# A hybrid decoder layer on one core: half 1's attention projection moved beside the memory attention, with later ticks for the norms

## The chip, the cores and the metric

The kernel runs on one NeuronCore of one Trainium2 chip. TensorE (PE) multiplies matrices, VectorE (DVE), ScalarE (ACT) and GpSimd (POOL) work on tiles, SyncE (SP) issues the weight loads; POOL issues the other transfers. The metric is device time in microseconds (us) of the whole kernel, the median of several runs.

## The reference, cut to what matters

```python
f = swiglu(rms_norm(x, g1), w_gate, w_up, w_down); x = x + 0.5 * rms_norm(f, p1)
h = rms_norm(x, mix_pre_g)
proj = h @ w_in              # columns: gated DeltaNet q,k,v,z,a,b | attention q,k,v
o_a = gdn_mixer(...)         # 4 heads x 128, chunked delta rule
o_b = dilated_mixer(...)     # 8 heads x 64, three (window, dilation) branches
x = x + rms_norm(concat(o_a, o_b) @ w_out, mix_post_g)
x = x + rms_norm(memory_cross_attention(rms_norm(x, mem_pre_g), rms_norm(mem, mem_kv_g)), mem_post_g)
f = swiglu(rms_norm(x, g2), w_gate2, w_up2, w_down2); x = x + 0.5 * rms_norm(f, p2)
```

x is 1024 tokens by 1024 channels in float32; the inner width of the two FFNs is 2816; memory has 256 tokens. All is float32.

## The kernel before

**Granules.** The tokens are worked in two halves of 512 (half 0 and half 1). Every large product is split into *granules*: one 512 KB piece of a weight matrix, loaded by SP into a ring of three, copied by ACT to a rounded part `w_hi` (L1247) and subtracted by DVE to a rest `w_lo` (L1652). PE forms hi·hi + hi·lo + lo·hi, 24 matmuls of 512 columns for a granule, into one of four PSUM banks called `acc` (column granules, `cgran`, L829 to L831; row granules, `rgroup`, L854 to L856). There are 386 granules in one fixed order, the list `STAGES` (L69 to L76): a name such as `up010a` is FFN 0, half 1, chunk 0, part a; `mix1` is all of w_in for half 1 (29 granules), `q0` and `o0` the query and output products of half 0's memory attention, `out1` the product with w_out.

**Ticks.** Everything that is latency-bound is a *job*, a generator that each engine has in its own version: the norms, the mixer (delta rule, then banded attention) and the memory attention. While an engine works through its granules it advances the current job by one `tick` at fixed places: PE two or three times in a granule (`sub`, `KCUT`, `CUTS`), ACT and DVE behind their part of that granule's w_hi and w_lo. `finish()` runs the rest of a job at once, with no granule matmuls between. The job's PE work goes to four other banks, `side`. An engine's instructions run strictly in this order, so a job's matmul that waits stops the granules behind it.

**Norms.** `norm(r, q)` first adds the result r to x and takes the sums (one tick for each of four token tiles, and three more), then in eight ticks transposes (PE L893), scales (ACT L1416) and subtracts (DVE L1820). `ready(q)` waits for its end before the granules that use it.

**Mixer.** `mixer(h)` has 3 ticks `ab`, 20 ticks for each of 4 chunks (k = 0 to 19), then the last gate, loads, 32 attention units, four `pair` transposes and two `conv` ticks: 129 ticks for half 0 and 162 for half 1, where a unit takes two. In a chunk, k = 2 transposes the output of the chunk before: POOL takes a root (L644), DVE multiplies (L1876), PE transposes (L916, `output_tr`, L913), DVE gates (L1880); then k = 3 goes on with L949. `conv` writes the operand of the product with w_out (ACT L1503, L1506, DVE L2022), and PE waits for it with `pe.wait_ge(delta["mix_lo"], ...)` (L1164, L1187).

**Order around half 1's projection.** PE runs `mix1` with the norm in front of it, `q0` with `mixer(1)` at three ticks a granule, then

```python
            for _ in memory(0, A):
                tick()
```

that is 19 ticks of memory attention in the `acc` banks, each with one of the mixer and no granule; `o0` with mixer ticks; 15 ticks of `norm(3, 6)`, again each with one of the mixer and no granule; then FFN 2 of half 0 (`ffn(1, ha, 0, 2, 2, 3)`, two ticks in an up granule and three in a down granule) with the mixer.

Of the kernel before, what the change touches and what calls it, by code (L numbers as in the profile page):

```python
# [18 lines left out]
ALU = mybir.AluOpType  # L19
# [38 lines left out]
MIX_PARTS = [("c", 12, 1, "a"), ("c", 4, 1, "a"), ("c", 1, 1, "a"), ("c", 8, 1, "ad"), ("r", 4, TT, "adad")]  # L58
# [53 lines left out]


# [18 lines left out]
Q0_SUB = 3  # L132
O0_SUB = 3


def mixer_ticks(h):
    t = [("ab", k, 0) for k in range(3)]
# [26 lines left out]
def hybrid_layer(nc, t):  # L164

    ctx = ExitStack()
    with ctx:
# [53 lines left out]
        qm = (at("qm0", [P, KT, TOK], HA), at("qm1", [P, KT, TOK], CZ))  # L221
        kmT = (at("km0", [P, KT, NMEM], HA + 16 * K), at("km1", [P, KT, NMEM], CZ + 16 * K))
        vm = (at("vm0", [P, 2, D], HA + 24 * K), at("vm1", [P, 2, D], CZ + 24 * K))
# [56 lines left out]
        def norm_ticks(r, q):  # L280
            nt = PRE_TILES[q] if q is not None else TT
            return nt + (3 if r is not None and q is not None else 1)
# [37 lines left out]
        mem_kv_in = sem("mem_kv_in")  # L320
        bias_made = sem("bias_made")
# [85 lines left out]

        def staged(eng, h):

            eng.wait_ge(qkv_stored, 16 * TT * (h + 1))  # L410
            for k in range(3):
                eng.wait_ge(slot_stored[k], 16 * (h + 1) * (3, 3, 2)[k])
# [5 lines left out]
        def _(sp):  # L418
# [75 lines left out]
        def _(pool):  # L494
# [115 lines left out]
            def qkv_store(h):  # L610

                i0 = START[f"mix{h}"] + 17
                for j in range(8):
                    na, nd = EVC[BANK[i0 + j]]
                    pool.wait_ge(acc_act, na)
                    pool.wait_ge(acc_dve, nd)
                    dst = q_dram if j < 4 else k_dram
                    pool.dma_start(dst[h][:, j % 4, :], stage_of[h][:, 4 + j % 3, :]).then_inc(slot_stored[j % 3], 16)
                for k in range(TT):
                    na, nd = EVC[TURNS[f"mix{h}"][k]]  # L620
                    pool.wait_ge(acc_act, na)
                    pool.wait_ge(acc_dve, nd)
                    pool.dma_start(v_dram[h][k], stage_of[h][:, k, :]).then_inc(qkv_stored, 16)
# [84 lines left out]

            keep(pool.memset(half_pow[:], -0.5))
# [25 lines left out]
            qkv_store(0)  # L735
# [7 lines left out]
            pool.wait_ge(pe_done, DONE[START["mix1"] - 1])  # L743
            for _ in norm(2, 5):
                pass

            qkv_store(1)
            pool.wait_ge(pe_done, DONE[START["q0"] - 1])
            pool.wait_ge(kv_made, 32)
            pool.dma_start(kmT[0][:], km_dram).then_inc(mem_kv_in, 16)  # L750
            pool.dma_start(vm[0][:], vm_dram).then_inc(mem_kv_in, 16)
            job[0] = mixer(1)
            tick(Q0_SUB * KT)
# [7 lines left out]
            for _ in norm(3, 6):  # L761
                tick()
# [1396 lines left out]
```

## Time and profile before

| | |
|---|---|
| median of three runs | 2729.25 us (2726.69 to 2729.84) |
| time of the profiled execution | 2725.15 us |
| its span, first to last instruction | 2723.4 us |
| PE busy | 2583.1 us, 95% |
| DVE, ACT, POOL busy | 1222.6, 949.7, 392.9 us |
| mean granted TensorE clock | 0.976 |

The page gives busy time by engine; since matmuls are pipelined, a busy PE is not one at its peak. The granted clock is 1.0 at 2.4 GHz and 0.5 at 1.2 GHz, so a mean between tells how much of a stretch ran at the lower level. In the views below a bracket or a column "idle before" gives how long the engine stood before an instruction and which one released it.

### The profile page before, as it was taken

To read this page: it belongs to the slowest core of one execution; us is meant where nothing else is said; L and a number is where in the kernel's file an instruction comes from. 1 tells how busy PE (TensorE), PEld (TensorE's weight loads), DVE (VectorE), ACT (ScalarE), POOL (GpSimd) and SP (SyncE) were. 2 spreads that over 40 slices of the span, in tenths; PEclk is the share of its full clock that TensorE was granted. 3 is DMA by queue.
4 is the path that set the end of the run, shared out by engine and by line. 5 is a ranking of instruction groups with operands and counts; after the bars stand their busy time and mean duration, and the time that the engine had idled before them with its cause. 6 is when DMAs were issued, how large, how long until landed. Compare 5 with 4: busy or idle time off the path is not lost.

```text
span 2723.4 us, 30946 instructions
## 1 busy us (share of the span) xinstructions
PE 2583.1 (95%) x12464; PEld 2113.1 (78%) x12464; DVE 1222.6 (45%) x1913; ACT 949.7 (35%) x1413; POOL 392.9 (14%) x485
## 2 busy tenths in 40 slices
PE   7999998999899999998998978999999999999996
PEld 7788887877778777786777766777787877888885
DVE  5543335634443444467345544333335435533333
ACT  5422224323232244554222223535434424322221
POOL 1460002002211210031022233000002002100001
PEclk9999999999999999999999988999999999999998
DMA  6543334343122233253430114222134234533331
GB/s 201 179 163 100 93 100 139 93 113 97 55 58 68 62 132 101 74 174 86 127 121 24 60 56 142 75 78 85 55 93 150 83 108 147 170 100 94 101 93 62
DMA packets 318846, 280.01 MB, mean 103 GB/s; under 512 B 12272, under 2 KB 266224, under 8 KB 317680
## 3 DMA queue, kind: packets, MB, share of 16 engines
q1 hardware_dynamic: 297856, 204.56, 25.2%
q0 software_dynamic: 19808, 73.46, 7.5%
q8 instruction: 100, 1.64, 0.2%
q14 instruction: 42, 0.34, 0.0%
q10 hardware_dynamic: 1040, 0.00, 0.0%
HBM read 248.63 MB, written 29.36 MB: 102 GB/s over the span
## 4 chain that ended last, share of the span: by engine, by line
PE 87%; DVE 5%; POOL 4%; issue 2%; DMA 1%; ACT 1%; SPq 0%; ACTq 0%; POOLq 0%; DVEq 0%
PE acc L829 15%; PE acc L831 15%; PE acc L830 15%; PE acc L854 9%; PE acc L856 8%; PE acc L855 8%; PE side L1027 3%; PE side L1053 2%; PE side L967 2%; PE side L982 1%; PE side L1042 1%; PE side L893 1%; POOL rs_pre L551 1%; PE side L973 1%; DMA cT<-v_dram 1%
## 5 line engine op out<-in xcount | busy, mean ns | idle before, releaser
L1652 DVE TENSOR_TENSOR w_lo<-w_raw,w_hi 128x1024 fp32r<-128x1024 f32 x384 | 474.0, 1235 | 614.2 <-ACT w_hi L1247 613.7
L1247 ACT ACTIVATE w_hi<-w_raw 128x1024 fp32r<-128x1024 f32 x384 | 405.4, 1056 | 580.4 <-PE acc L856 318.9
L829 PE MATMUL acc<-ha_hi,w_hi 128*128 128x512 f32 (+2 forms) x968 | 392.4, 405 | 1.3 <-DVE ha_lo L1820 1.3
L829 PE MATMUL acc<-hb_hi,w_hi 128*128 128x512 f32 (+1 forms) x968 | 378.3, 391 | 1.2 <-DVE w_lo L1652 1.2
L831 PE MATMUL acc<-hb_hi,w_lo 128*128 128x512 f32 (+1 forms) x968 | 377.4, 390 | 0.0
L830 PE MATMUL acc<-hb_lo,w_hi 128*128 128x512 f32 (+1 forms) x968 | 377.3, 390 | 0.0
L831 PE MATMUL acc<-ha_hi,w_lo 128*128 128x512 f32 (+2 forms) x968 | 376.1, 388 | 0.0
L830 PE MATMUL acc<-ha_lo,w_hi 128*128 128x512 f32 (+2 forms) x968 | 374.7, 387 | 0.0
L854 PE MATMUL acc<-w_hi,act_hi 128*128 128x512 f32 x704 | 286.3, 407 | 0.0
L856 PE MATMUL acc<-w_lo,act_hi 128*128 128x512 f32 x704 | 276.1, 392 | 0.0
L855 PE MATMUL acc<-w_hi,act_lo 128*128 128x512 f32 x704 | 275.4, 391 | 0.0
L829 PEld LDWEIGHTS acc<-ha_hi,w_hi 128*128 128x128 f32 (+1 forms) x968 | 184.6, 191 | 52.5 <-issue 17.6
L831 PEld LDWEIGHTS acc<-ha_hi,w_lo 128*128 128x128 f32 (+1 forms) x968 | 183.7, 190 | 39.1
L829 PEld LDWEIGHTS acc<-hb_hi,w_hi 128*128 128x128 f32 (+1 forms) x968 | 181.5, 187 | 40.0 <-DVE w_lo L1652 1.6
L831 PEld LDWEIGHTS acc<-hb_hi,w_lo 128*128 128x128 f32 (+1 forms) x968 | 181.3, 187 | 39.1
L830 PEld LDWEIGHTS acc<-hb_lo,w_hi 128*128 128x128 f32 (+1 forms) x968 | 181.4, 187 | 38.3
L830 PEld LDWEIGHTS acc<-ha_lo,w_hi 128*128 128x128 f32 (+1 forms) x968 | 184.6, 191 | 33.1 <-issue 0.5
L854 PEld LDWEIGHTS acc<-w_hi,act_hi 128*128 128x128 f32 x704 | 133.0, 189 | 36.9 <-issue 10.9
L856 PEld LDWEIGHTS acc<-w_lo,act_hi 128*128 128x128 f32 x704 | 132.7, 188 | 28.9
L855 PEld LDWEIGHTS acc<-w_hi,act_lo 128*128 128x128 f32 x704 | 133.1, 189 | 26.6 <-issue 1.4
L549 POOL TENSOR_SCALAR rs_post<-ssq_post 128x1 f32<-128x1 f32 x32 | 15.1, 473 | 723.1 <-ACT junk_z L1389 720.3
L1951 DVE CUSTOM_DVE_ANT_0 arena<-side,arena 128x512 f32<-128x512 f32 (+2 forms) x96 | 51.0, 556 | 148.9 <-PE side L1027 145.3
(329 smaller groups left out, 3506.5 us busy)
## 6 DMA issues: line engine op xcount, KB each, us to landing
w_raw<-in_ffn_w_gate SPq DMA_DIRECT2D x88, 512.0 KB, 3.7
w_raw<-in_ffn_w_up SPq DMA_DIRECT2D x88, 512.0 KB, 3.7
w_raw<-in_ffn_w_down SPq DMA_DIRECT2D x88, 512.0 KB, 3.3
w_raw<-in_w_in SPq DMA_DIRECT2D x56, 512.0 KB, 3.8
x_dram<-xbuf POOLq DMA_DIRECT2D x24, 512.0 KB, 3.0
xbuf<-x_dram POOLq DMA_DIRECT2D x24, 512.0 KB, 5.9
arena<-bias_dram POOLq DMA_DIRECT2D x16, 512.0 KB, 3.6
w_raw<-in_w_out SPq DMA_DIRECT2D x16, 512.0 KB, 3.3
```

Of the source, the lines that this page charges most:

```text
L829: pe.matmul(out, hi[:, k, 0:m], xh[:, k, 0:n], start=(k == 0), stop=False)
L830: pe.matmul(out, hi[:, k, 0:m], xl[:, k, 0:n], start=False, stop=False)
L831: done = pe.matmul(out, lo[:, k, 0:m], xh[:, k, 0:n], start=False, stop=(k == KT - 1))
L854: pe.matmul(out, xh[:, kk, ts], hi[:, k, :], start=(kk == 0), stop=False)
L855: pe.matmul(out, xl[:, kk, ts], hi[:, k, :], start=False, stop=False)
L856: done = pe.matmul(out, xh[:, kk, ts], lo[:, k, :], start=False, stop=(kk == 2 * n - 1))
L967: mm = pe.matmul(pairs_of(SB[0][:, hs], s, 1), arena[:, A_S[v % 2], hs], pairs_of(arena[:, U_, hs], s, 1), start=True, stop=True)
L1027: mm = pe.matmul(score_bank(h, n, hh)[:, 0:m], qbT[rows, p, i * P:(i + 1) * P], k_ring(p)[rows, hh, 0:m], start=True, stop=True)
L1053: mm = pe.matmul(SB[3][:, out_cols(n)], pt_of(n)[:, c * P:(c + 1) * P], v_ring(hd // 2)[:, c, (hd % 2) * AD:(hd % 2 + 1) * AD], start=(c = ...
L1247: act.activation(w_hi[:, j % RING, :], w_raw[:, j % RING, :], ACT.Copy).then_inc(w_hi_ok, 1)
L1652: dve.tensor_tensor(w_lo[:, j % RING, :], w_raw[:, j % RING, :], w_hi[:, j % RING, :].bitcast(F32), ALU.subtract).then_inc(w_lo_ok, 1)
L1951: ins = dve.tensor_tensor_reduce(sbuf[:, hh * TOK:hh * TOK + m], score_bank(h, n, hh)[:, 0:m], bias[:, b0 + hh * TOK:b0 + hh * TOK + m], 1 ...
```

## The change

`mix` is cut in three: `gdn_in` (17 granules), `qk_in` (6) and `kv_in` (2 column granules and a group of 4 row granules). For half 0 they still follow one another. For half 1 the order is now gdn_in, q0, qk_in, o0, kv_in. `memory(0)` runs as the job beside qk_in, at three ticks a granule, in the `side` banks and without the mixer; the norm behind it, `norm(3, 6)`, and the mixer advance together (`both`) beside kv_in at two ticks a granule, and `finish()` runs what is left of that norm. FFN 2 of half 0 then has three ticks in an up granule and two in a down granule.

Keys and values of memory come in pieces into a small ring in xbuf's space (`memory_loads` on POOL); q, k and v of half 1 pass through three slots of `arena`, each freed by its store (`slot_free`); queries of half 0's memory attention lie in oT's space.

Four norms get idle ticks between their sums and their transposes (`SLACK`: 6 for q = 2, 5 and 8, 5 for q = 6). The mixer gets one idle tick before its third `ab` tick (so 130 and 163 ticks). In a chunk the output transpose moves from k = 2 to k = 5, DVE's product for it from k = 1 to k = 4 and the gate from k = 2 to k = 6, in another bank. `up010` is cut after 4 blocks of two granules rather than 3, with two ticks a granule in front of the cut. The norm q = 8 is finished behind dn103 rather than in front.

```diff
-STAGES += [("up010a", up_parts(3)), ("mix0", MIX_PARTS), ("up010b", up_parts(3)), ("dn010", dn_parts(0))]
+STAGES += [("up010a", up_parts(4)), ("gdn0", GDN_PARTS), ("qk0", QK_PARTS), ("kv0", KV_PARTS), ("up010b", up_parts(2)), ("dn010", dn_parts(0))]
...
-STAGES += [("out0", ROW_PARTS), ("mix1", MIX_PARTS), ("q0", [("c", KT, 1, "ad")]), ("o0", ROW_PARTS)]
+STAGES += [("out0", ROW_PARTS), ("gdn1", GDN_PARTS), ("q0", [("c", KT, 1, "ad")]), ("qk1", QK_PARTS),
+           ("o0", ROW_PARTS), ("kv1", KV_PARTS)]
...
+SLACK = {2: 6, 5: 6, 6: 5, 8: 6}
...
-    t = [("ab", k, 0) for k in range(3)]
+    t = [("ab", 0, 0), ("ab", 1, 0), ("idle", 0, 0), ("ab", 2, 0)]
...
+            def both(first, second):
+                for _ in first:
+                    next(second, None)
+                    yield
...
@@ PE, chunk(l, k)
                         chan(1, QN)
-                        if l:
-                            output_tr(n - 1, l - 1)
...
                             tr.then_inc(delta["T_psum"], 1)
+                        elif l:
+                            output_tr(n - 1, l - 1)
...
@@ PE, the order of the work
-            up(ha, 3, 3)
+            up(ha, 4, 2)
             finish()
             ready(3)
-            mix(hb, 2)
+            gdn_in(hb, 2)
+            qk_in(hb, 2)
+            kv_in(hb, 2)
             pe.wait_ge(mask_st, N_CONST)
             job[0] = mixer(0)
-            up(ha, 3, 3)
+            up(ha, 2, 3)
...
-            for _ in memory(0, A):
-                tick()
+            job[0] = memory(0)
+            qk_in(ha, 3)
+            finish()
             pe.wait_ge(memo["out_lo"], 8)
+            job[0] = mix_job
             for _ in range(2):
                 rgroup(hc, 4, TT, O0_SUB)
-            for _ in norm(3, 6):
-                tick()
+            job[0] = both(norm(3, 6), mix_job)
+            kv_in(ha, 2)
+            emptied(TURNS["kv1"][-1])
+            finish()
             ready(6)
-            ffn(1, ha, 0, 2, 2, 3)
+            job[0] = mix_job
+            ffn(1, ha, 0, 2, 3, 2)
             finish()
             pe.wait_ge(delta["mix_lo"], 4)
```

In the excerpts below a row is the line, the operation, what it writes and reads, and its shape; line numbers are each version's own (before: L829 to L831 and L854 to L856 are granules; after: L907 to L909 and L932 to L934).

The first place is PE in chunk 3 of half 1. Before, the transpose of the last chunk's output (L916) stands right behind the transposes of keys and queries (L910).

```order
L855 MATMUL acc<-w_hi,hc_lo 128x512
L856 MATMUL acc<-w_lo,hc_hi 128x512
L910 MATMUL side<-ident,arena 128x128 x8
L916 MATMUL side<-ident,cT 128x128 x4
L854 MATMUL acc<-w_hi,hc_hi 128x512
```

After, it is L1002 and stands behind the first product of the chunk's inversion (L1049), three ticks later.

```order
L908 MATMUL acc<-ha_lo,w_hi 128x512
L909 MATMUL acc<-ha_hi,w_lo 128x512
L1049 MATMUL side<-arena 128x32x2 x4
L1002 MATMUL side<-ident,cT 128x128 x4
L907 MATMUL acc<-ha_hi,w_hi 128x512
```

The second place is PE at the end of half 0's mixer. Before, the last transposes (L1089) have granules of the down product (act_hi) on both sides, 156 more granule matmuls up to the next transposes of a norm, of which the first 60 are still of this down product.

```order
L855 MATMUL acc<-w_hi,act_lo 128x512
L856 MATMUL acc<-w_lo,act_hi 128x512
L1089 MATMUL side<-ident,arena 128x128 x4
L854 MATMUL acc<-w_hi,act_hi 128x512
L855 MATMUL acc<-w_hi,act_lo 128x512
```

After, the last of the down product stands in front of the end of the attention (L1128, L1139) and of these transposes (L1175), and the next row is the product with w_out, whose operand (hb) `conv` writes.

```order
L933 MATMUL acc<-w_hi,act_lo 128x512
L934 MATMUL acc<-w_lo,act_hi 128x512
L1128 MATMUL side<-ident,arena 128x128 x4
L1139 MATMUL side<-cT,arena 128x64 x7
L1175 MATMUL side<-ident,arena 128x128 x4
L932 MATMUL acc<-w_hi,hb_hi 128x512
L933 MATMUL acc<-w_hi,hb_lo 128x512
```

The third place is PE at norm(3, 6). Before, mixer ticks of chunk 3 follow each other without a granule from k = 3 (L949, L950) on, and behind seven of them the norm's transposes (L893) come between.

```order
L950 MATMUL side<-cT 128x128
L956 MATMUL side<-ident,arena 128x128 x4
L967 MATMUL side<-arena 128x32x2 x4
L982 MATMUL side<-arena 128x32x2 x4
L967 MATMUL side<-arena 128x16x4 x4
L973 MATMUL side<-ident,arena 128x128 x4
L982 MATMUL side<-arena 128x16x4 x4
L967 MATMUL side<-arena 128x8x8 x4
L973 MATMUL side<-ident,arena 128x128 x4
L982 MATMUL side<-arena 128x8x8 x4
L893 MATMUL acc<-ident,oT 128x128 x4
```

After, granules of kv_in stand in front of the norm's first transpose (L979), and only its eight ticks are without a granule; the mixer is then at the end of chunk 2 (L1066 at k = 16, L1078 at k = 17) and goes on to k = 3 of chunk 3.

```order
L933 MATMUL acc<-w_hi,ha_lo 128x512
L934 MATMUL acc<-w_lo,ha_hi 128x512
L1049 MATMUL side<-arena 128x64 x4
L1055 MATMUL side<-ident,arena 128x128 x4
L979 MATMUL acc<-ident,oT 128x128 x4
L1066 MATMUL side<-arena 128x64 x4
L979 MATMUL acc<-ident,oT 128x128 x4
L1078 MATMUL side<-state,cT 128x128
```

## Rows read from the trace of the kernel before

**Rows 1.** The page, parts 1, 4 and 5: busy time, chain by engine, one group.

```profile
PE 2583.1 (95%) x12464; PEld 2113.1 (78%) x12464; DVE 1222.6 (45%) x1913; ACT 949.7 (35%) x1413; POOL 392.9 (14%) x485
...
PE 87%; DVE 5%; POOL 4%; issue 2%; DMA 1%; ACT 1%; SPq 0%; ACTq 0%; POOLq 0%; DVEq 0%
...
L1247 ACT ACTIVATE w_hi<-w_raw 128x1024 fp32r<-128x1024 f32 x384 | 405.4, 1056 | 580.4 <-PE acc L856 318.9
```

**Rows 2.** Windows (length; busy PE, PEld, DVE, ACT, POOL; clock): mix0; half 1's attention.

```profile
487.00:644.00 157.00, 157.00 (x694) 127.63 (x693) 76.53 (x112) 47.81 (x65) 5.42 (x10) 1.00 0.39 109
...
1665.00:2001.00 336.00, 331.90 (x1653) 255.41 (x1653) 128.19 (x335) 152.68 (x222) 17.53 (x30) 0.99 0.28 90
```

**Rows 3.** Waits of PE, whole span: us in total, times, longest.

```profile
PE side L916 <- DVE cT L1876: 22.0, 6, 5.1
PE side L893 <- DVE oT L1813: 20.1, 3, 10.4
...
PE side L956 <- DVE arena L1913: 10.7, 8, 3.2
...
PE side L1027 <- DMA cT<-v_dram: 5.6, 2, 3.9
PE side L893 <- DVE xbuf L1813: 5.5, 2, 4.6
PE side L893 <- DVE res_cz L1813: 5.2, 2, 2.6
PE side L1067 <- DVE sm L1992: 4.4, 2, 2.2
```

**Rows 4.** Timeline of chunk 2 of half 0: start, us, engine, line.

```profile
809.30 1.01 POOL L644 TENSOR_TENSOR sm<-sm,half_pow 128x4 f32<-128x4 f32 x1
...
810.34 1.52 DVE L1876 TENSOR_TENSOR cT<-cT,sm 128x512 f32<-128x512 f32 x1 [4.65 <-POOL sm L644]
...
811.92 0.69 PE L916 MATMUL side<-ident,cT 128*128 128x128 f32 x2 [5.07 <-DVE cT L1876]
```

**Rows 5.** Windows around three waits.

```profile
439.00:487.00 48.00, 39.60 (x182) 32.49 (x181) 29.11 (x32) 24.52 (x37) 19.30 (x24) 0.89 0.47 152
...
808.00:816.00 8.00, 4.08 (x13) 3.41 (x14) 3.35 (x3) 2.37 (x3) 3.15 (x4) 0.57 0.00 0
1208.00:1246.00 38.00, 27.56 (x114) 22.49 (x113) 29.79 (x41) 19.41 (x30) 14.01 (x21) 0.87 0.43 130
```

**Rows 6.** Timeline of DVE in the norm q = 3, which starts at 439.

```profile
450.53 1.28 DVE L1802 SCALAR_TENSOR_TENSOR oT<-oT,rs_post,grow_z 128x1024 f32<-128x1024 f32 x1
...
462.06 0.74 DVE L1813 TENSOR_SCALAR oT<-xbuf,rs_pre 128x1024 f32<-128x1024 f32 x1
```

**Rows 7.** Windows: memory attention of half 0; norm(3, 6).

```profile
1457.00:1527.00 70.00, 60.00 (x335) 46.95 (x335) 40.98 (x103) 25.55 (x71) 17.89 (x16) 0.93 0.00 1
...
1613.00:1665.00 52.00, 33.22 (x194) 29.77 (x193) 31.05 (x39) 16.21 (x29) 25.31 (x31) 0.69 0.14 52
1621.00:1652.00 31.00, 18.39 (x85) 16.90 (x84) 18.66 (x21) 10.07 (x20) 18.52 (x23) 0.50 0.22 86
```

**Rows 8.** Timeline at the end of half 0's mixer.

```profile
1144.97 0.27 PE L1089 MATMUL side<-ident,arena 128*128 128x128 f32 x1
...
1145.61 0.60 ACT L1498 ACTIVATE cT<-side 128x512 f32<-128x512 f32 x1 [2.98 <-PE side L1089]
...
1149.39 1.90 ACT L1506 ACTIVATE hb_hi<-cT 128x2048 fp32r<-128x2048 f32 x1
...
1152.58 2.29 DVE L2022 TENSOR_TENSOR hb_lo<-cT,hb_hi 128x2048 fp32r<-128x2048 f32 x1
```

**Rows 9.** ACT at 1671; groups of ACT, 1665 to 1838.

```profile
1672.25 1.28 ACT L1317 ACT_TABLE_LOAD   x1
1673.55 0.60 ACT L1317 ACTIVATE sg<-acc 128x512 f32<-128x512 f32 x1
...
L1459 ACT ACTIVATE arena<-arena,sm 128x640 f32<-128x640 f32 (+3 forms) x17 | 16.7, 982 | 41.2 <-DVE sm L1959 41.2
```

More of the change, by code:

```diff
@@ L281, in norm_ticks @@
             nt = PRE_TILES[q] if q is not None else TT
-            return nt + (3 if r is not None and q is not None else 1)
+            return nt + (3 if r is not None and q is not None else 1) + SLACK.get(q, 0)
         gain_in = [sem("gain_in_mem"), sem("gain_in_ffn1")]
@@ L734, in _ @@
             x_next(t["x"][0], 1, 0, 3)
-            qkv_store(0)
+            for n in range(12):
+                qkv_store(0, n)
             for _ in mixer(0):
@@ L808, in chain, with both @@
                     yield from j
+            def both(first, second):
+                for _ in first:
+                    next(second, None)
+                    yield
             def bank_free(n):
@@ L871, in dn, with gdn_in, qk_in, kv_in @@
                     rgroup((act_hi, act_lo), CH[c] // 2, TT, sub, blk[0] - CH[c])
-            def mix(op, sub):
-                for j in range(25):
+            def gdn_in(op, sub):
+                for j in range(17):
                     cgran(op, sub, TOK, 8 if j == 16 else P)
+            def qk_in(op, sub):
+                for _ in range(6):
+                    cgran(op, sub)
+            def kv_in(op, sub):
+                for _ in range(2):
+                    cgran(op, sub)
                 rgroup(op, 4, TT, sub)
@@ L1236, in chain, with both @@
                     yield from j
+            def both(first, second):
+                for _ in first:
+                    next(second, None)
+                    yield
             def split(j):
@@ L1287, in cplain, with rgroup @@
                     pend[0] = out
-            def rgroup(n, tiles, sub, dst_of):
+            def rgroup(n, tiles, sub, dst_of, before=None):
                 for j in range(n):
@@ L1574, in _ @@
             flush()
-            mix(1, 2)
+            gdn_in(1, 2)
             finish()
             flush()
-            job[0] = mixer(1)
+            mix_job = mixer(1)
+            job[0] = mix_job
             cplain(KT, Q0_SUB, lambda j: qm[0][:, j, :])
             flush()
-            for _ in memory(0, A):
-                tick()
+            job[0] = memory(0)
+            qk_in(1, 3)
+            finish()
+            job[0] = mix_job
             rows_to(oT, 4, O0_SUB)
             flush()
-            for _ in norm(3, 6):
-                tick()
-            ffn(0, 2, 2, oT, 3)
+            job[0] = both(norm(3, 6), mix_job)
+            kv_in(1, 2)
+            flush()
+            finish()
+            job[0] = mix_job
+            ffn(0, 2, 3, oT, 2)
             finish()
@@ L1642, in chain, with both @@
                     yield from j
+            def both(first, second):
+                for _ in first:
+                    next(second, None)
+                    yield
             def split(j):
@@ L1805, in norm @@
                                                  op0=ALU.mult, op1=ALU.add).then_inc(post_x, 1)
-                    if q is not None and s > off:
+                    if q is not None and off < s <= nt + off:
                         k = s - off - 1
@@ L2094, in _ @@
             flush()
-            mix(1, 2)
+            gdn_in(1, 2)
             finish()
             flush()
-            job[0] = mixer(1)
+            mix_job = mixer(1)
+            job[0] = mix_job
             cplain(KT, Q0_SUB, lambda j: qm[0][:, j, :])
             flush()
-            for _ in memory(0, A):
-                tick()
+            job[0] = memory(0)
+            qk_in(1, 3)
+            finish()
+            job[0] = mix_job
             rows_to(oT, 4, O0_SUB)
             flush()
-            for _ in norm(3, 6):
-                tick()
-            ffn(0, 2, 2, oT, 3)
+            job[0] = both(norm(3, 6), mix_job)
+            kv_in(1, 2)
+            flush()
+            finish()
+            job[0] = mix_job
+            ffn(0, 2, 3, oT, 2)
             finish()
```

243 lines of the change are left out of this document (155 added, 88 removed).

## The prediction

> **What bounds the kernel now.** I read the page first: PE is busy 95% of the span and makes 87% of the chain that ended last [rows 1]. Busy is not yet full speed, so I then looked for a stretch that shows what dense work costs: in mix0, 694 matmuls fill 157.00 us at granted clock 1.00 [rows 2], 0.226 us each, and 5.43 us for a granule of 24. The change adds no granule. So its worth lies in what PE loses beside that work, and that has two parts. The first is waits: the waits of PE name them with their releasers [rows 3]. The second comes with them: behind a wait of some 4 us the windows show a stretch at half clock. Around the longest wait for an output transpose it is 0.57 over 8 us, that is 2 x 0.43 x 8 = 6.9 us at 1.2 GHz, of which the wait itself covers about half; the other 3.6 us are work done at half speed, 1.8 us lost [rows 5]. I price each wait so: its length, and half of what PE works in the low stretch.
>
> **The change, gains first.**
>
> (a) *Output transposes.* PE waits for them 22.0 us in 6 waits [rows 3]. The reason is seen in the timeline: POOL's root stands behind three large products, DVE's product (1.52 us) waits for it 4.65 us, and PE 5.07 us for that [rows 4]. Three ticks later the same chain, which overran by 5.1 us at most, has 5.4 to 8.2 us of granules more in front of it, so the wait goes. Five of the waits drew a low stretch at 1.8 us: 22 + 9 = 31. The next step of the chunk still waits for DVE (L956, 10.7 us in 8, [rows 3]) and starts earlier now; I take 2 us back. Gain 29, bounds 12 (half of each wait turns up at L956, and its clock) and 31.
>
> (b) *Norm q = 5.* The longest wait is 10.4 us, 38.0 minus 27.6 in its window, where clock 0.87 means 9.9 us at half speed, about half of it work: 2.5 lost [rows 3, 5]. Six idle ticks at two a granule are 16.3 us, more than the wait. Gain 13.
>
> (c) *Norms q = 2 and q = 8.* 4.6 us and 2.6 us of waits [rows 3], the same cure; with their low stretches 7 and 4. Gain 11.
>
> (d) *Norm q = 3.* It has no slack, but its ticks come two a granule. Before, PE idled 8.4 us here (48.0 minus 39.6, [rows 5]); DVE's last product ended at 462.8 [rows 6], 23.5 us behind the norm's start. PE will now ask for it at the eighth tick, four granules or 21.7 us on: 1.7 us of wait if the chain keeps its pace. It may not: a tile takes 2.5 us of DVE in two products like the one shown, and the last product now stands in the fourth granule's first tick, behind that granule's w_lo. The wait lies between 1.7 and 7.1 (one granule later). I take 5. Gain 3, bounds 1 and 9.
>
> (e) *The idle tick in ab.* 4.4 us in 2 waits (L1067, [rows 3]); a further tick is 1.4 to 2.7 us. With clock, gain 6.
>
> (f) *Memory attention.* Its window of 70 us has 10.0 us of idle PE, and clock 0.93 (9.8 us at half speed, of which I count 7 as work): 13.5 lost, 1.2 of it an output transpose that (a) has [rows 7]. Beside granules 18 of 19 ticks are covered. Left are the last tick and the wait behind it: each an ACT copy like the 0.60 us one [rows 8], a DVE subtraction of 0.7, and hand-overs, 1.9 us, so 4; a low stretch 2; the start (queries just copied, keys just loaded) 1. Gain 5, bounds 0 and 11.
>
> (g) *norm(3, 6).* Of 52 us PE idles 18.8, and from 1621 to 1652 all of its 18.4 us of work ran at 0.50, 9.2 lost: 28 [rows 7]. After, four tiles at 2.5 us on DVE delay mixer ticks beside kv_in: 2. The last v tile waits for a slot's store, and PE for its copy: 2. Then eight ticks stand bare. The fifteen bare ticks of before idled 18.8, or 1.25 each, so 10; since k = 17 to 19 and 0 to 3, each waiting for the one before, are among them, I take 12, and 5 for the clock. Together 21. Gain 7, bounds -5 and 20.
>
> Gains: 29 + 13 + 11 + 3 + 6 + 5 + 7 = 74.
>
> **Then what it costs.**
>
> (h) *End of half 0's mixer.* Before, 6 granules of three ticks in each of up010b and dn010 and 48 of two are 132 ticks for 129. Now up010b has 4: 12 + 18 + 96 = 126 for 130. Four ticks are bare: the last unit, pair, both conv; and the row behind them is the product that waits for conv. This cover is what hid it: before, the chain from the pair transposes (1144.97) to the last subtraction (1152.58 + 2.29) took 9.9 us with a w_hi copy and a w_lo in it [rows 8] and 60 matmuls of the down product (13.6 us) ran meanwhile. Bare it is 0.45 + 0.3 + 0.60 + 2 x 1.90 + 0.2 + 2.29 = 7.6, with the last unit 2.5 ahead and 1.3 of PE's own work off: 8.8, and 2.4 for the clock as in (b). Cost 11, bounds 5 and 14. Queued behind it are all granules of out0.
>
> (i) *End of half 1's mixer.* 24 + 24 + 12 + 8 + 48 x 2 = 164 ticks for 163 (before 166 for 162). The pair transposes stand three ticks, 8.2 us, ahead of out1; the same chain with its w_hi and w_lo takes 9 to 10. Cost 1.
>
> (k) *Loads of the attention.* PE waited 3.9 us for them [rows 3]; three ticks of cover shrink from 8.2 to 5.4 us. Cost 3.
>
> (l) *Attention at three ticks beside up granules.* Before, this stretch lost 4.1 us in 336 [rows 2]. In an up granule with the gate ACT has, ahead of the copy that PE's second tick wants: table load 1.28, silu 0.60 [rows 9], w_hi 1.06 [rows 1], table load 1.28, exp 0.98 [rows 9], the copy 0.60 [rows 8], and 0.3 of hand-over: 6.1 us. PE comes there after 18 matmuls (4.1) and a tick of about 2: 6.1. That is level, in 12 granules, with 0 to 1.5 us of wait each. Cost 4, bounds 0 and 18.
>
> The Trainium skill, ScalarE: Activation LUTs, section What ACT_TABLE_LOAD costs, speaks against this step: it gives 1.28 us for the load and some 1.4 us more for a drain at each switch of set. The trace has the 1.28 us, but the silu starts at 1673.55, 0.02 us behind the load [rows 9], so no drain is paid here. By the page, (l) would be an estimated 33 us (12 x 2.8) and the sum 26.
>
> Costs: 11 + 1 + 3 + 4 = 19. Net 74 - 19 = 55. The profiled execution took 2725.15 us around a span of 2723.4; the sum makes 2670 and 2668 of these. It is 4.1 us under the median of the three runs; from that, 2729.25 - 55 = **2674 us**.
>
> **Rivals.**
>
> *The waits come back one step on.* (a) is worth 12: L956 and the A-block products of POOL wait for the same engines. For it: POOL still takes the root ahead of them. Against it: POOL is done with the root at 810.3, 1.6 us before PE even began that transpose [rows 4], and the product is now wanted three ticks later. Time 2674 + 17 = 2691.
>
> *Better cover than I give.* (h) 5, (l) 0, (d) 9, (f) 9: 6 + 4 + 6 + 4 = 20 us less, 2654.
>
> *Slower: the attention at three ticks.* If the second tick's wait in (l) falls into all 24 up granules, it costs 24 times its length against 59 us of everything else; it is no change at 2.5 us a granule and slower by over 0.2% from (59 + 5.5) / 24 = 2.7. At 3.0, both table loads and a bit on the path, the time is 2729 - 59 + 72 = 2742. For it: ACT's path is as long as PE's. Against it: gate granules are every second one, and dn100 had three ticks in the same stretch with clock 0.99 [rows 2].
>
> *A drain behind table loads,* as a mechanism of ACT in (l): 1.4 us more at each of two loads in 12 granules, 12 x 2.8 = 33 for 4, so 2703; the gap of 0.02 us speaks against it [rows 9]. It is the page's rule, weighed in (l).
>
> *The change does not bring what it names:* bare ticks in (g) as dear as before, and all small returns at their bound, 2715 to 2728. For it: from k = 0 to k = 2 the work goes from PE to ACT, DVE, POOL and DVE before PE has it again, and that stands bare.
>
> **How the numbers follow.** Forecast (2660 to 2688) 0.55; waits come back 0.21; better cover 0.12; little left 0.06; slower 0.04; drain 0.02. The range leaves out the slow rival, the end of little left, and the far ends of the two on either side: 2652 to 2706. A change under 0.2% (5.5 us) is about what a measurement of this kernel can't tell from none. Faster by more 0.93, within 0.03, slower 0.04.
>
> **What the profile after should show.** In the waits of PE the row for the output transposes near zero, and L956 not over 13 us in all; no wait at the norm's transposes of q = 2, 5 and 8, and one of 2 to 7 us at q = 3. Right ahead of out0, a wait of 8 to 9 us for DVE's hb_lo, which did not exist. In the bare ticks behind kv_in 8 to 14 us of waits, the largest for the normed queries at k = 2, and a granted clock under 0.8. The memory attention beside granules at clock near 1.0 but for its end. Most likely to make me wrong: waits at the transposed probabilities all through up100 and up101, or a low clock in the half of the mixer where I expect none.

## The result, and the profile after

The changed kernel takes 2646.80 us (median of 4 runs, 2645.15 to 2647.55) against 2727.97 us (4 runs, 2724.16 to 2729.84): ratio 0.9706, 95% interval 0.9694 to 0.9718, 81 us less. The forecast was 2674, range 2652 to 2706. The direction and most terms hold; the gain is 27 us larger than forecast.

The page of the changed kernel, the rows that answer to [rows 1]:

```profile
PE 2554.3 (97%) x12464; PEld 2090.3 (79%) x12464; DVE 1231.1 (47%) x1913; ACT 936.5 (35%) x1405; POOL 402.9 (15%) x491
...
PE 89%; DVE 5%; POOL 2%; issue 1%; DMA 1%; ACT 1%; SPq 0%; ACTq 0%; DVEq 0%; POOLq 0%
```

PE executes the same 12464 matmuls and is busy 28.8 us less: that is the time saved by matmuls that no longer run at half clock. The span of the profiled executions fell by 77.8 (2723.4 to 2645.6), so the other 49 us are waits.

The waits of PE in the changed kernel, whole span (us in total, times, longest), for [rows 3]:

```profile
PE side L979 <- DVE memx L1941: 11.3, 1, 11.3
PE side L1113 <- DMA cT<-v_dram: 8.3, 2, 7.4
PE side L996 <- DVE arena L2030: 7.2, 6, 3.7
PE side L1038 <- DVE arena L2039: 7.0, 8, 1.8
PE acc L932 <- DVE hb_lo L2148: 7.0, 1, 7.0
PE side L1049 <- DVE arena L2051: 5.1, 2, 2.7
PE side L979 <- DVE oT L1941: 4.4, 2, 2.6
PE side L979 <- DVE res_cz L1941: 2.6, 1, 2.6
```

L979, L1038, L1113 and L1002 are L893, L956, L1027 and L916 of before. The output transposes (22.0 us in 6) have no row any more. Their neighbour L956 (k = 4), which I expected to take some of it over, fell from 10.7 to 7.0. The norms' row for oT fell from 20.1 to 4.4 and the one for res_cz from 5.2 to 2.6. Those for xbuf (5.5 to 0.9) and for ab (4.4 to 0.3) stand further down now. New is hb_lo, 7.0 us in one wait ahead of out0. The loads of the attention grew from 5.6 to 8.3.

Windows of the changed kernel (length; busy PE, PEld, DVE, ACT, POOL; clock; DMA): the norm q = 3; the end of half 0's mixer; the norm q = 5; the memory attention beside granules; the eight bare ticks; the attention's loads; the up granules of chunk 1 of FFN 2 with the attention at three ticks.

```profile
433.00:485.00 52.00, 49.44 (x227) 40.43 (x226) 32.52 (x35) 27.32 (x40) 17.03 (x24) 0.97 0.50 160
1117.00:1131.00 14.00, 6.09 (x30) 4.89 (x29) 7.46 (x8) 7.92 (x9) 2.78 (x5) 0.76 0.12 35
1179.00:1207.00 28.00, 27.04 (x120) 22.06 (x118) 23.27 (x29) 17.41 (x28) 13.52 (x21) 1.00 0.48 151
1347.00:1415.00 68.00, 65.47 (x279) 48.27 (x277) 31.89 (x83) 25.67 (x66) 6.07 (x10) 1.00 0.27 86
1543.00:1569.00 26.00, 18.02 (x136) 16.31 (x136) 15.53 (x24) 11.24 (x18) 10.39 (x12) 0.93 0.10 38
1630.00:1645.00 15.00, 7.64 (x22) 4.84 (x20) 2.45 (x7) 2.21 (x4) 4.00 (x7) 0.66 0.84 302
1746.00:1881.00 135.00, 135.00 (x702) 102.30 (x701) 51.23 (x159) 68.67 (x106) 4.18 (x7) 1.00 0.22 67
```

Read against [rows 5] and [rows 7]: in the memory attention clock 0.93 became 1.00; in the stretch behind o0, 0.69 became 0.93. Only two windows are still low, the end of half 0's mixer and the attention's loads. The last row is dense throughout.

**Where the 78 us came from.** I gave each matmul of both traces the median interval to its successor for matmuls of its kind; what a stretch takes beyond the sum is its loss. (The figures hold to about 1 us, since they depend a little on what counts as one kind; the gains hold better.) The losses of the whole program are 164.6 us before and 86.4 after. By stretch, beside the forecast's terms sorted into the same stretches:

| Stretch | lost before | after | gain | forecast |
|---|---|---|---|---|
| norm q = 2 | 8.9 | 2.0 | 6.9 | 7 |
| norm q = 3 | 10.7 | 4.3 | 6.4 | 3 |
| half 0's mixer to up013 | 41.5 | 13.5 | 28.0 | 20 |
| dn013 and out0 | 2.4 | 13.6 | -11.2 | -11 |
| norm q = 5 | 11.8 | 0.7 | 11.1 | 13 |
| q0 and memory attention | 22.6 | 7.2 | 15.4 | 9 |
| o0, norm(3, 6), bare ticks | 46.1 | 22.2 | 23.9 | 18 |
| chunks 0 and 1 of FFN 2, half 0 | 9.3 | 15.3 | -6.0 | -8 |
| norm q = 8 | 4.2 | -0.5 | 4.7 | 4 |

For the third row the forecast has three output transposes with their clock (12.9 + 5.4), half of (e), and 1 taken back. The surplus sits where the mixer runs beside granules: 8 us in half 0 and 12 in the two stretches of half 1.

### The profile page after: what moved, and what is told of

Read it like the earlier page. It is cut to its first block, busy times and chain, and to the rows that moved or that the text cites. A ratio compares the mean times of both kernels' runs of the same rounds, so it can differ in the third digit from the quotient of the medians.

```text
span 2645.6 us, 30948 instructions
## 1 busy us (share of the span) xinstructions
PE 2554.3 (97%) x12464; PEld 2090.3 (79%) x12464; DVE 1231.1 (47%) x1913; ACT 936.5 (35%) x1405; POOL 402.9 (15%) x491
## 4 chain that ended last, share of the span: by engine, by line
PE 89%; DVE 5%; POOL 2%; issue 1%; DMA 1%; ACT 1%; SPq 0%; ACTq 0%; DVEq 0%; POOLq 0%
PE acc L907 16%; PE acc L909 15%; PE acc L908 15%; PE acc L932 9%; PE acc L934 9%; PE acc L933 9%; PE side L1113 3%; PE side L1139 2%; PE side L1049 1%; PE side L1066 1%; PE side L1128 1%; PE side L1191 1%; PE side L1223 1%; PE side L979 1%; POOL rs_pre L590 1%
## 5 line engine op out<-in xcount | busy, mean ns | idle before, releaser
L1775 DVE TENSOR_TENSOR w_lo<-w_raw,w_hi 128x1024 fp32r<-128x1024 f32 x384 | 488.2, 1272 | 542.5 <-ACT w_hi L1355 542.1
L907 PE MATMUL acc<-ha_hi,w_hi 128*128 128x512 f32 (+2 forms) x968 | 396.0, 409 | 2.8 <-DVE ha_lo L1948 1.1
L907 PE MATMUL acc<-hb_hi,w_hi 128*128 128x512 f32 (+1 forms) x968 | 377.6, 390 | 1.2 <-DVE w_lo L1775 1.2
L909 PE MATMUL acc<-hb_hi,w_lo 128*128 128x512 f32 (+1 forms) x968 | 376.7, 389 | 0.0
L909 PE MATMUL acc<-ha_hi,w_lo 128*128 128x512 f32 (+2 forms) x968 | 374.2, 387 | 0.0
L932 PE MATMUL acc<-w_hi,act_hi 128*128 128x512 f32 x704 | 285.4, 405 | 0.0
L934 PE MATMUL acc<-w_lo,act_hi 128*128 128x512 f32 x704 | 275.1, 391 | 0.0
L907 PEld LDWEIGHTS acc<-ha_hi,w_hi 128*128 128x128 f32 (+1 forms) x968 | 183.3, 189 | 53.1 <-issue 18.6
L909 PEld LDWEIGHTS acc<-ha_hi,w_lo 128*128 128x128 f32 (+1 forms) x968 | 182.6, 189 | 38.9
L907 PEld LDWEIGHTS acc<-hb_hi,w_hi 128*128 128x128 f32 (+1 forms) x968 | 180.9, 187 | 40.1 <-DVE w_lo L1775 1.9
L909 PEld LDWEIGHTS acc<-hb_hi,w_lo 128*128 128x128 f32 (+1 forms) x968 | 180.9, 187 | 38.6
L932 PEld LDWEIGHTS acc<-w_hi,act_hi 128*128 128x128 f32 x704 | 132.3, 188 | 37.7 <-issue 12.2
L934 PEld LDWEIGHTS acc<-w_lo,act_hi 128*128 128x128 f32 x704 | 132.1, 188 | 28.7
```

The costliest lines, as they stand in the source:

```text
L907: pe.matmul(out, hi[:, k, 0:m], xh[:, k, 0:n], start=(k == 0), stop=False)
L909: done = pe.matmul(out, lo[:, k, 0:m], xh[:, k, 0:n], start=False, stop=(k == KT - 1))
L932: pe.matmul(out, xh[:, kk, ts], hi[:, k, :], start=(kk == 0), stop=False)
L934: done = pe.matmul(out, xh[:, kk, ts], lo[:, k, :], start=False, stop=(kk == 2 * n - 1))
L1775: dve.tensor_tensor(w_lo[:, j % RING, :], w_raw[:, j % RING, :], w_hi[:, j % RING, :].bitcast(F32), ALU.subtract).then_inc(w_lo_ok, 1)
```

## The experiments

"Before" is 2726.6 to 2728.4 us in all groups of runs; each ratio is to the runs of before on the same chip, with its 95% interval.

**1. Output transposes alone**, on the kernel before (the edit in short; the transposes also go to another bank).

```diff
# PE, chunk step k
-  k == 2: output_tr(n - 1, l - 1)      k == 3: wait gated
+  k == 5: output_tr(n - 1, l - 1)      k == 17: wait gated
# DVE
-  k == 1: out_norm(n - 1, l - 1)       k == 2: out_gate(n - 1, l - 1)
+  k == 4: out_norm(n - 1, l - 1)       k == 6: out_gate(n - 1, l - 1)
```

> The kernel before, with the output transposes alone moved three steps later in the chunk (their norm and their gate with them). The priced theory (each wait costs its length and half of the work in the half-clock stretch behind it) gives 29 to 33 us less than before: 22.0 of waits, 9 of clock, and nothing or 2 us lost at the step that waits for the normed queries. If the miss of 27 us in the forecast sits in this term (the transposes held back more than their own waits), it gains 45 us or more. If the waits come back one step on, 12 to 17.

Measured 2694.80, ratio 0.9879 (0.9865 to 0.9894), 34 us less. Its profiled span is 28.4 shorter than before's, and by stretch the loss falls 41.5 to 23.8 in half 0's mixer and 46.1 to 33.6 behind the memory attention. Two of its waits of PE:

```profile
PE side L952 <- DVE arena L1911: 11.7, 8, 3.2
PE side L963 <- DVE arena L1923: 11.6, 4, 7.2
```

These two lines are L956 and L967 of before. The first, the next step, grew by 1.0 and the second by 1.2 (from 10.4 in 4). Term (a), 29, holds.

**2. No idle ticks for the norms**, on the changed kernel.

```diff
-SLACK = {2: 6, 5: 6, 6: 5, 8: 6}
+SLACK = {6: 5}
```

> The changed kernel without the idle ticks of the norms q = 2, 5 and 8 (those of q = 6, which pace the merged stretch, stay). The forecast's terms (b) and (c) give 24 us more than the changed kernel, about 2671, with waits at the norm transposes of about 10, 5 and 3 us back. If a wait costs its length alone and the clock is no part of it, 18 us. If the miss sits here, 35 or more.

Measured 2669.91, ratio 0.9791 (0.9775 to 0.9808): 23 us slower than the changed kernel. Its row for the norms reads

```profile
PE side L979 <- DVE oT L1941: 14.7, 3, 10.3
```

The 10.3 us wait is back in full. Terms (b) and (c), 24 together, hold with length plus clock; length alone (18) does not.

**3. The regrouping alone:** the changed kernel with transposes as before, SLACK as in 2, and

```diff
-    t = [("ab", 0, 0), ("ab", 1, 0), ("idle", 0, 0), ("ab", 2, 0)]
+    t = [("idle", 0, 0), ("ab", 0, 0), ("ab", 1, 0), ("ab", 2, 0)]
```

> The changed kernel with everything but the regrouping undone: output transposes back at their old step, no idle ticks for q = 2, 5 and 8, the idle tick of ab put ahead of ab where it parts nothing. What is left is the move of the query, key and value projections of half 1 and the ticks that follow from it. The forecast's terms for it (5 + 7 gained, 19 lost) make it 7 us slower than the kernel before. From the trace of the changed kernel I now expect it 6 to 12 us faster: the memory attention keeps 4 us of waits at full clock, the bare ticks 8 us, and the attention at three ticks costs nothing. If the surplus sits in the other parts, it is within 3 us of the 7 slower.

Measured 2706.19, ratio 0.9919 (0.9904 to 0.9933): 22 us faster than before. Both numbers that I had given, 7 slower and 6 to 12 faster, were wrong. By stretch, 14 us of gain stand in half 0's mixer (41.5 to 27.7), where nothing of the order changes but the place of one block of two granules, and where the output transposes still wait.

**4. The end of half 0's mixer covered**, on the changed kernel, in all three engines.

```diff
-            ffn(0, ha, 1, 4, 2)
+            ffn(0, ha, 1, 2, 2)
+            ffn(0, ha, 2, 3, 2, 3)
+            ffn(0, ha, 3, 4, 2)
```

> The changed kernel with three ticks a granule instead of two in the six down granules of chunk 2 in half 0: 132 ticks for the 130 that the mixer wants, so that none stands bare ahead of out0. If term (h) is right (a bare chain of 7 to 9 us and its clock), the 7.0 us wait for hb_lo goes and the time falls by 8 to 11 us, to about 2637. Rival: three ticks a granule in the attention are dearer in waits than in a down granule of half 1 (0.7 us), and it gains under 4.

Measured 2638.58, ratio 0.9672 (0.9657 to 0.9686): 8 us less than the changed kernel. The row for hb_lo is gone, the loss of dn013 and out0 falls from 13.6 to 2.8, and that of dn012 grows from 2.2 to 3.3. Term (h), 11, holds: 10.8 in the trace. The rest of the way to 8 is given back elsewhere: up100 loses some 2 us more than in the changed kernel and up102a, with the norm q = 7, 1.6.

**5. The split of chunk 0 alone**, on the kernel before (the order in short).

```diff
-up010a 3 blocks at 3 ticks, mix0, up010b 3 blocks at 3 ticks
+up010a 4 blocks at 2 ticks, mix0, up010b 2 blocks at 3 ticks
```

> The kernel before with one thing of the change: chunk 0 of half 0 is split 4 and 2 blocks around the mixer projection instead of 3 and 3, the four blocks at two ticks a granule. Nothing of half 1 moves, no idle tick, transposes at their old step. The forecast's terms (d) 3 gained and (h) 11 lost give 8 us slower than before. My theory now is that the shift of two ticks against the granules takes waits and low clock out of the delta chunks of half 0, 14 us that no term of the forecast held, beside 6.5 gained at the norm q = 3 and 12 lost ahead of out0: 8 us faster than before. If the gain seen in the regrouping alone comes from half 1 only, this one is 5 or more slower.

Measured 2726.35, ratio 0.9995 (0.9986 to 1.0005): no difference. By stretch: q = 3 gains 6.4 (the forecast's 3), dn013 and out0 lose 11.3 (11), and the delta chunks of half 0 gain 2 only. My theory that the shift by two ticks explains experiment 3 fell. Experiment 3 differs from this one in half 0 by one thing, the idle tick ahead of ab.

**6. Four more bare ticks**, on the changed kernel.

```diff
-SLACK = {2: 6, 5: 6, 6: 5, 8: 6}
+SLACK = {2: 6, 5: 6, 6: 9, 8: 6}
```

> The changed kernel with four more idle ticks in the norm q = 6, so that twelve ticks of the mixer stand bare behind the value projection instead of eight. By the forecast's price (1.5 us of wait and 0.6 of clock for a bare tick) 8 us slower than the changed kernel; by what the trace after shows (0.96 us each, hardly any clock) 4 us; less still by 1 to 3 where the later ticks beside FFN 2 are relieved, as the mixer is four ticks further on. If bare ticks draw the clock down once they are many, as in the kernel before (fifteen of them with all work of 30 us at 0.50), 12 us or more, with a granted clock near 0.5 in the stretch.

Measured 2657.04, ratio 0.9739 (0.9725 to 0.9754): 10 us slower than the changed kernel. The window of its bare ticks:

```profile
1543.00:1583.00 40.00, 28.07 (x168) 25.75 (x167) 20.65 (x31) 11.39 (x20) 15.28 (x16) 0.79 0.04 15
```

Before the four ticks, 26 us held 8.0 of idle PE at clock 0.93; now 40 us hold 11.9 at 0.79. A further bare tick costs 1.0 us of wait, but the granted clock is lower, and the loss of the stretch grows by 10.6 from 19.5. So the price of a bare tick is not constant. That their number sets it is argued and not shown, since other steps of the mixer stand bare too (k = 4 to 7 are added).

**7. One idle tick for q = 3, 4 and 7**, on experiment 4.

```diff
-SLACK = {2: 6, 5: 6, 6: 5, 8: 6}
+SLACK = {2: 6, 3: 1, 4: 1, 5: 6, 6: 5, 7: 1, 8: 6}
```

> The kernel with the covered end (three ticks in the down granules of chunk 2, half 0) and one idle tick each for the norms q = 3, 4 and 7, whose transposes still wait 2.6, 1.8 and 2.6 us. Sixteen ticks for sixteen. If the waits and their clock go, 9 us less than with the covered end alone, about 2630. Rival: the last transpose now stands in the last tick, and the copy and the subtraction behind it (0.6 + 0.7 us and hand-overs) stand bare ahead of the next granule, which gives 1.5 to 2 us back at each of three: 4 us or less gained.

Measured 2633.97, ratio 0.9656 (0.9640 to 0.9672): 4.6 us less than experiment 4. The rival is right, as two rows of its waits show:

```profile
PE acc L907 <- DVE hb_lo L1952: 3.1, 2, 1.6
PE acc L907 <- DVE ha_lo L1952: 2.6, 2, 1.6
```

Three waits of 1.56 us stand now where the last transpose's copy and subtraction are bare, in place of 2.6, 1.8 and 2.6. By stretch, against experiment 4, q = 3 and q = 7 gain 2.5 each, while out0, with the norm q = 4, loses 1 us more: that one is not worth its tick.

**8. Cover for the attention's loads**, on experiment 4.

```diff
-    t += [("load", k, 0) for k in range(2)]
+    t += [("load", k, 0) for k in range(2)] + [("idle", 0, 0)] * (3 * h)
-            ffn(1, ha, 0, 2, 3, 2)
+            ffn(1, ha, 0, 1, 3, 2)
+            ffn(1, ha, 1, 2, 3, 3)
```

> The kernel with the covered end and, in half 1, three idle ticks between the loads of the attention and its first scores, paid with three ticks in the six down granules of chunk 1 of FFN 2. If term (k) is the wait of 7.4 us for the keys and values and some 4 us of clock behind it, both go, and it takes 10 to 11 us less than the covered end alone, about 2628. Rival: the down granules at three ticks cost 3 or more, or the loads are slow because they wait for their turn in the queue, not for their length, and a wait stays.

Measured 2632.69, ratio 0.9651 (0.9636 to 0.9665): 5.9 us less than experiment 4, half of what I expected.

```profile
PE side L1113 <- DMA cT<-v_dram: 3.3, 2, 2.6
```

The wait fell from 7.8 to 2.6, not to nothing; the loss of up100 fell from 14.0 to 6.4, and up101 lost 1.0 more. The loads themselves did not change much: the last transfer waited for takes 8.5 us from its issue in the kernel before, 8.1 in the changed one and 8.8 here. It is the cover that differs.

**9 and 10. One idle tick in the kernel before**, ahead of ab, and between its ticks.

```diff
-    t = [("ab", k, 0) for k in range(3)]
+ 9: t = [("idle", 0, 0), ("ab", 0, 0), ("ab", 1, 0), ("ab", 2, 0)]
+10: t = [("ab", 0, 0), ("ab", 1, 0), ("idle", 0, 0), ("ab", 2, 0)]
```

> The kernel before with one idle tick put ahead of the first tick of ab, in both halves; it parts nothing, it only shifts every later tick of the mixer by one against the granules (133 minus 3 is 130 ticks for 132 in half 0, 163 for 166 in half 1). My theory now: this shift alone, not the parting of the ab ticks, takes waits and low clock out of the delta chunks, since at two ticks a granule the odd one falls elsewhere: 12 us less in the chunks of half 0, 3 to 10 in half 1, together 15 to 22 less than before. By the forecast's term (e), which counted only the two ab waits, this kernel is worth nothing, 0 to 2.

> The kernel before with the idle tick where the change has it, between the second and the third tick of ab. The forecast's term (e) says 6 us less than before (4.4 of ab waits and clock). My theory now says this comes on top of the shift: 4 to 6 less than the kernel with the idle tick ahead, 20 to 27 less than before.

Measured 2715.13, ratio 0.9951 (0.9935 to 0.9968), and 2708.93, ratio 0.9933 (0.9918 to 0.9948): 13 and 19 us less than before, each a little short of what my theory gave (15 to 22, and 20 to 27). The parting is worth about 6, as term (e) said. The mere shift by one tick is worth 13 by the medians and 8.2 by the profiled spans, and no term had it. Waits of PE from up010b to up012 in the kernel before:

```profile
PE side L916 <- DVE cT L1876: 12.9, 3, 5.1
PE side L910 <- DVE arena L1902: 4.6, 3, 2.8
PE side L956 <- DVE arena L1913: 3.8, 4, 1.8
```

and in experiment 9:

```profile
PE side L916 <- DVE cT L1876: 9.3, 3, 4.0
PE side L956 <- DVE arena L1913: 3.2, 4, 1.8
...
PE side L910 <- DVE arena L1902: 1.3, 2, 1.0
```

Same work, same steps, 7.5 us less in these rows (a new wait of 0.7 aside): only the place of each step in its granule differs.

**11. No idle tick in half 0**, on the changed kernel.

```diff
-    t = [("ab", 0, 0), ("ab", 1, 0), ("idle", 0, 0), ("ab", 2, 0)]
+    t = [("ab", 0, 0), ("ab", 1, 0)] + [("idle", 0, 0)] * h + [("ab", 2, 0)]
```

> The changed kernel without the idle tick in half 0 only. By term (e) the one ab wait of 2.2 us and its clock come back (3 us) and one bare tick fewer ahead of out0 gives 2 back: 1 us slower. By the shift theory the chunk waits of half 0 come back too, smaller than in the kernel before since the output transposes are out of the way: in all 6 to 10 us slower, about 2654.

Measured 2653.69, ratio 0.9733 (0.9719 to 0.9748): 7 us slower than the changed kernel, where term (e) gives 1. The loss of half 0's mixer is 19.3 instead of 13.5. dn013 and out0 lose the same 13.6: one bare tick fewer there gives nothing back. Of what the mixer loses, some 3.4 stand in up010b, where the ab ticks are, 2.5 in dn010, and nothing in the granules with two ticks. So part of the 7 is the parting, and with the output transposes out of the way the shift is worth less than in the kernel before.

**12. Combined:** the edits of experiments 4, 7 and 8.

> The covered end, the idle ticks for the norms q = 3, 4 and 7, and the cover for the attention's loads, together on the changed kernel. Each alone on the covered end gave 4.6 and 5.9 us; they lie in different stretches, so 10 us less than the covered end alone and 18 to 19 less than the changed kernel, 2627 to 2629. If the shift of two times one tick in half 1 (more idle ticks) costs elsewhere, 2632.

Measured 2627.64, ratio 0.9635 (0.9621 to 0.9650): 19 us less than the changed kernel, as expected. It is the fastest of all, at clock 0.995.

**13 and 14. Two and three idle ticks ahead of ab**, on the kernel before.

```diff
-    t = [("ab", k, 0) for k in range(3)]
+    t = [("idle", 0, 0)] * 2 + [("ab", k, 0) for k in range(3)]      # 14: * 3
```

> The kernel before with two idle ticks ahead of ab in both halves (131 ticks for 132 in half 0, 164 for 166 in half 1). If it is the odd or even place of each step in the granule that decides, the chunk steps fall as in the kernel before: within 4 us of before, 2724 to 2731. If any later start helps, as much as one idle tick or more: 2715 or less.

> The kernel before with three idle ticks ahead of ab (132 for 132, 165 for 166). By odd and even, as with one: about 2715, with up to 4 us more where the end of half 0's mixer now stands right ahead of out0. If any later start helps: 2712 or less. If one was a coincidence of single waits: near 2728.

Measured 2729.82, ratio 1.0010 (1.0001 to 1.0020), and 2728.74, ratio 1.0011 (1.0001 to 1.0021). Two ticks take the gain back, as odd and even would have it. Three don't bring it again; by its number this is what I had written down for a coincidence, near 2728. By stretch, from up010b to up012, the losses with 0, 1, 2 and 3 idle ticks are 37.2, 30.1, 40.6 and 31.8. But with three the ends come late, as this row of the waits of PE shows,

```profile
PE acc L854 <- DVE hb_lo L2022: 6.8, 2, 3.7
```

ahead of out0 and of out1. Those two ends lose 12 us more than with one idle tick.

Odd and even is not the whole rule either. Part the same stretch by ticks a granule (to about 1 us):

| Idle ticks | 0 | 1 | 2 | 3 |
|---|---|---|---|---|
| up010b and dn010, three ticks a granule | 19 | 15 | 22 | 19 |
| up011 to up012, two ticks a granule | 20 | 15 | 19 | 14 |

The loss returns when the shift is a whole granule: three ticks in the first row, two in the second. A later start by itself would not do that; the place of the steps in their granule does. Of the 22, 3.3 is one wait of the ab ticks that is longer with two idle ticks (L1067, 5.5 in place of 2.2). In half 1 nothing of the kind is seen: q0 to the norm(3, 6), where most waits stand in bare ticks, lose 70, 68, 68 and 66.

**15. The bare ticks at another place:** experiment 12 with

```diff
-            kv_in(ha, 2)        SLACK[6] = 5
+            kv_in(ha, 3)        SLACK[6] = 11
```

and the down granules of chunk 1 of FFN 2 at two ticks again.

> The combined kernel with three ticks a granule instead of two in the six granules of the key and value projection of half 1 (eleven idle ticks in the norm q = 6), and two again in the down granules of chunk 1 of FFN 2: 170 ticks for 167. Eight ticks stand bare as before, but they are k = 2 to 9 of the last chunk, not k = 16 to 19 and 0 to 3. The forecast's price for eight bare ticks, 1.5 us each, names no place; the trace shows 0.96 each. If the steps from k = 17 to 3 are what makes them dear (the normed queries), it takes 4 to 6 us less than the combined kernel. If each bare tick costs the same, no difference. Rival: three ticks beside a granule of the value projection wait for DVE, and it is 3 us slower.

Measured 2641.00 (2634.27 to 2641.13), ratio 0.9681 (0.9666 to 0.9695): 13 us slower than experiment 12. Its timeline at the value projection's last tile (start, us, engine, line):

```profile
1544.81 2.22 POOL L715 TENSOR_TENSOR sm<-sm,half_pow 128x8 f32<-128x8 f32 x1
...
1547.01 1.26 POOL L718 TENSOR_TENSOR arena<-arena,tri_s 128x512 f32<-128x512 f32 x1
...
1550.85 1.01 POOL L700 TENSOR_TENSOR sm<-sm,half_pow 128x4 f32<-128x4 f32 x1
1551.81 1.69 POOL L656 DMA_DIRECT2D v_dram<-arena  x3
1554.16 0.69 DVE L1809 COPY arena<-acc 128x512 f32<-128x512 f32 x1 [5.67 <-DMA v_dram<-arena]
...
1554.95 1.09 PE L979 MATMUL acc<-ident,oT 128*128 128x128 f32 x4 [9.56 <-issue]
```

A miss, and not by any theory that I gave. POOL issues the stores of the v tiles, and six ticks further on its root and masks (k = 0 and 1) stand ahead of them in its queue. DVE's copy of the last tile waits for a slot's store. PE stands 9.56 us; the view names no releaser, but the kernel has PE wait there for that copy (`emptied`), and PE starts as it ends. In the changed kernel PE waits 1.2 us at this place. By stretch, the 13 us stand from o0 to these bare ticks. What the place of the bare ticks does to their price is left open by this run.

## Why the prediction was right in direction and 27 us short

- *(a) Output transposes, 29:* right. 28 in the profiled span, 34 by the medians. In experiment 1, 2.2 us of waits came back at L956 and L967, the 2 that I had taken. The row for the transposes is gone, as foretold.
- *(b), (c) norms q = 5, 2, 8, 24:* right. 23 by experiment 2; 11.1, 6.9 and 4.7 in the table.
- *(d) Norm q = 3, 3:* too small. I took 5 us of wait between 1.7 and 7.1; it is 2.6, and the gain 6.4, inside the bounds.
- *(e) The idle tick, 6:* **the step that failed.** I priced what it parts, 4.4 us of ab waits, and put the rest at nothing, as if every other step of the mixer kept its wait. But it also moves every later step of the mixer by one tick against the granules. Alone in the kernel before, the tick is worth 19, of which 13 are the shift; undone in half 0 of the changed kernel it costs 7, where the term gives 1. The same sentence failed for the regrouping, which shifts half 1's steps too: experiment 3, forecast by my terms at 4 to 7 slower than before, is 22 faster, and 13 of those are the idle tick ahead of ab, if its worth is the same there as alone.
- *(f) Memory attention, 5 (0 to 11):* mechanism right, price too high. I left 4 of wait, 2 of clock, 1 of start. There are 1.5 and 1.4 us of wait, at the two places named, and the window's clock is 1.00; the stretch of qk1 loses 3.9 where I had left 7.
- *(g) norm(3, 6), 21 left:* about right, 19.5. The waits in the bare ticks are 8, at the low end of 8 to 14. The largest (L996, 3.7) is at the normed queries of k = 2, as named, but the clock is 0.93 where I expected under 0.8. Experiment 6 shows what I had carried over wrongly: a clock loss taken from fifteen bare ticks is not the same share for each tick of eight.
- *(h) End of half 0's mixer, 11:* right. 7.0 of wait (8 to 9 foretold), and 10.8 gone when it is covered. (i), 1: no wait for hb_lo ahead of out1 is seen.
- *(k) Attention's loads, 3:* too small. The longest wait grew from 3.9 to 7.4, with its clock, and up100 loses some 5 us more than before. In experiment 8 three ticks more take 5.2 us off that wait.
- *(l) Attention at three ticks, 4:* nothing. 135.0 us of 135 are busy at clock 1.00, and that stretch lost 1.2. This rules out the slower rival (a wait of 3.0 in each up granule). It also rules out the rival of the drain. By the Trainium skill, ScalarE: Activation LUTs, section What ACT_TABLE_LOAD costs, about 1.4 us more are due at each switch. The trace does not agree. In one of these granules ACT's work stands back to back around both loads:

```profile
1756.09 0.28 ACT L1577 ACTIVATE arena<-side 128x128 f32<-128x128 f32 x1 [2.69 <-PE side L1128]
1756.39 1.28 ACT L1427 ACT_TABLE_LOAD   x1
1757.68 0.60 ACT L1427 ACTIVATE sg<-acc 128x512 f32<-128x512 f32 x1
1758.18 1.05 ACT L1355 ACTIVATE w_hi<-w_raw 128x1024 fp32r<-128x1024 f32 x1
1759.25 1.28 ACT L1569 ACT_TABLE_LOAD   x1
1760.54 1.04 ACT L1569 ACTIVATE arena<-arena,sm 128x896 f32<-128x896 f32 x1
```

All 12 loads between 1746 and 1881 start 0.02 us behind the instruction ahead of them, and ten of them end 0.01 us before the next one (the other two are followed by ACT waiting for its input). No 1.4 us has room on either side.

The pieces nearly add up: transposes 33.6, norms 23.1, idle tick 18.8, and the regrouping without the shift 9.6 (22.2 less 12.6) are 85; together they give 81, so 4 overlap. The forecast had 29, 24, 6 and -4. The surplus is 4.6, 12.8 and 13.6, less 0.9 and the overlap. Part of the 13.6 is placed, (d) with 3.4, (f) with 3 to 5 and (l) with 3, while (k) took some 2 more than forecast; the rest isn't settled. The last 1.3 us of the 27 is the starting point: the forecast counts from 2729.25, and before measured beside the change is 2727.97.

The rivals that forecast less (waits come back, little left, slower, drain) all fell. "Better cover than I give", 2654, was nearest, by (d), (f) and (l), but one of its two largest parts, (h) at 5, was wrong, and it did not hold what the shift gave. That it came near is in part luck.

## What to carry to other kernels

In a schedule where one stream of steps is dealt out over the granules of another, an inserted or removed tick is never local: list on which part of a granule each waiting step falls before and after, down to the end of the stream. Then try the insertion by itself, and by one and two ticks more: here one tick changed the loss of one stretch by 7 to 11 us, the gain came and went with a period of one granule, and the ends could take it back. A bare chain at the end of such a stream was priced well by adding its links. Where an engine computes and also issues stores (POOL here), moving its steps needs the list of what then stands ahead of those stores.

## What the hardware showed that I had not expected

Whether a wait draws the clock down is not told by its length alone. Four windows of 4 us of the changed kernel, behind or around waits of 2.56, 2.75, 2.38 and 3.73 us:

```profile
458.00:462.00 4.00, 4.00 (x13) 3.13 (x12) 3.08 (x4) 2.26 (x3) 1.92 (x4) 0.57 1.05 313
1508.00:1512.00 4.00, 4.00 (x24) 3.18 (x23) 3.51 (x5) 2.94 (x6) 3.67 (x5) 1.00 0.32 133
1520.00:1524.00 4.00, 4.00 (x12) 3.10 (x12) 3.66 (x4) 0.98 (x2) 3.29 (x3) 0.59 0.28 103
1564.00:1568.00 4.00, 3.52 (x17) 3.29 (x18) 1.08 (x2) 1.86 (x4) 3.83 (x6) 0.57 0.01 4
```

The longest but one, 2.75, left the clock at 2.4 GHz; behind 2.38 us most of the 4 us ran at 1.2 GHz. The same step behaves otherwise in another run: in experiment 12 it waits 2.71 us, and the 4 us behind it (1497 to 1501) have a clock of 0.59. In the kernel before, the two ab waits are 2.20 us each, the first ending at 652.66, the second at 1391.2:

```profile
652.50:656.50 4.00, 3.84 (x25) 3.42 (x26) 1.14 (x6) 2.53 (x6) 0.00 (x0) 1.00 0.02 4
...
1392.00:1396.00 4.00, 4.00 (x15) 3.23 (x14) 2.19 (x6) 1.85 (x5) 0.00 (x0) 0.57 0.47 154
```

What decides between them is not settled here. A low stretch of this kind is worth 4 x 0.43 = 1.7 us, so a forecast that gives one to every wait, or to none, errs by that at each.
